# Modulation rows of two MLPs: four column blocks summed over partitions at once, on four column groups of the array, and turned

## The reference, cut to what matters

```python
mod_l = [m[:, None, :] for m in jnp.split(s_lat @ ada_w[i] + ada_b[i], N_MOD, axis=-1)]   # 1024 x 6144
...
h_lat = h_lat + mod_l[5] * _sq_relu_mlp(
    _modulate(_rmsnorm(h_lat, norm2_g[i]), mod_l[3], mod_l[4]), mlp_w1[i], mlp_w2[i])
...
mod = jax.nn.silu(c) @ w_ada[l] + b_ada[l]                                                # second block
```

## Time and profile before

| what | value |
|---|---|
| median of three runs | 2590.87 us (2590.12 to 2594.27) |
| the profiled execution, its own time | 2594.25 us |
| its span in the profile | 2592.4 us |
| mean granted clock of TensorE | 0.961 |
| TensorE busy | 2382.4 us, 92% |
| VectorE busy | 1006.2 us, 39% |
| ScalarE busy | 620.6 us, 24% |
| GpSimd busy | 112.4 us, 4% |
| HBM traffic | 592.5 MB, 229 GB/s over the span |

### The profile page before, as it was taken

The page is one execution under the profiler, slowest core; times in us unless marked ns, Lnnn a source line. Parts: engine busy times, 40 slices in busy tenths (PEclk is TensorE's granted clock), DMA queues, the critical chain, the costliest instruction groups (busy, mean ns, idle before and its releaser), DMA issues.

```text
span 2592.4 us, 23747 instructions
## 1 busy us (share of the span) xinstructions
PE 2382.4 (92%) x9961; PEld 1394.2 (54%) x9961; DVE 1006.2 (39%) x1616; ACT 620.6 (24%) x1002; POOL 112.4 (4%) x120
## 2 busy tenths in 40 slices
PE   5999988899999999999789979799898989989888
PEld 2445544588888788888667737333232323233222
DVE  4555463366663666564556372301111011101011
ACT  2112163333223333233446464110000000000000
POOL 2000000000000000000221312000000000000000
PEclk8999988999999999999899999899999999999999
DMA  9312330355553145550211203599999999999997
GB/s 352 105 65 81 109 118 0 114 182 190 174 184 128 49 163 195 195 179 33 89 49 33 94 29 130 215 427 429 431 430 432 430 431 431 431 430 432 429 431 316
DMA packets 121024, 594.04 MB, mean 229 GB/s; under 512 B 9346, under 2 KB 10880, under 8 KB 95318
## 3 DMA queue, kind: packets, MB, share of 16 engines
q1 hardware_dynamic: 117522, 583.23, 56.7%
q0 software_dynamic: 3088, 9.17, 1.0%
q10 hardware_dynamic: 308, 0.13, 0.0%
HBM read 590.37 MB, written 2.13 MB: 229 GB/s over the span
## 4 chain that ended last, share of the span: by engine, by line
PE 77%; DMA 12%; DVE 6%; ACT 3%; issue 1%; POOL 0%; DVEq 0%; ACTq 0%; POOLq 0%
PE PS L1150 15%; PE PS L840 9%; PE PS L842 9%; PE PS L841 9%; PE PS L656 8%; PE PS L891 5%; PE PS L149 5%; PE PS L1167 3%; DMA RING<-in_w_down_dram 3%; PE PS L1177 2%; PE PS L564 2%; DMA RING<-in_w_gate_dram 2%; PE PS L740 2%; DMA RB_a<-in_w_down_dram 2%; DMA RING<-in_w_up_dram 2%; PE PS L591 1%
## 5 line engine op out<-in xcount | busy, mean ns | idle before, releaser
L1150 PE MATMUL PS<-RING,HID_e 128*64 128x512 f32 x608 | 204.9, 607 | 9.1 <-DMA RING<-in_w_up_dram 4.7
L1150 PE MATMUL PS<-RB_a,HID_e 128*64 128x512 f32 x576 | 195.6, 598 | 5.2 <-DMA RB_a<-in_w_up_dram 4.5
L1150 PE MATMUL PS<-AT_g,HID_e 128*64 128x512 f32 x288 | 130.6, 601 | 5.1 <-DMA AT_g<-in_w_up_dram 4.2
L1150 PE MATMUL PS<-HID_e 128*64 128x512 f32 x288 | 130.8, 602 | 4.5 <-DMA HID_e<-in_w_gate_dram 2.7
L1150 PE MATMUL PS<-XT,HID_e 128*64 128x512 f32 x288 | 130.8, 602 | 4.3 <-DMA XT<-in_w_gate_dram 2.7
L2476 DVE TENSOR_TENSOR TMP<-TMP,PS 128x512 f32<-128x512 f32 x32 | 19.8, 683 | 284.6 <-PE PS L1150 284.6
L1167 PE MATMUL PS<-RING,HID_e 128*64 128x512 f32 x288 | 112.1, 656 | 13.0 <-DMA RING<-in_w_down_dram 13.0
L1696 ACT ACTIVATE PADS<-PS 128x512 f32<-128x512 f32 x8 | 4.8, 597 | 490.3 <-PE PS L149 490.3
L2484 DVE TENSOR_TENSOR HID_e<-PS,HID_e 128x512 f32<-128x512 f32 x16 | 10.3, 686 | 278.3 <-PE PS L1167 278.3
L1167 PE MATMUL PS<-RB_a,HID_e 128*64 128x512 f32 x304 | 107.3, 624 | 11.0 <-DMA RB_a<-in_w_down_dram 11.0
L1150 PEld LDWEIGHTS PS<-RING,HID_e 128*64 128x64 f32 x608 | 61.7, 139 | 97.7 <-issue 84.5
(11 more groups left out here) (448 smaller groups left out, 4712.9 us busy)
## 6 DMA issues: line engine op xcount, KB each, us to landing
RING<-in_w_gate_dram SPq DMA_DIRECT2D x19, 2048.0 KB, 22.0
RING<-in_w_up_dram SPq DMA_DIRECT2D x19, 2048.0 KB, 18.3
RB_a<-in_w_down_dram SPq DMA_DIRECT2D x19, 2048.0 KB, 21.6
RB_a<-in_w_gate_dram SPq DMA_DIRECT2D x18, 2048.0 KB, 22.4
RB_a<-in_w_up_dram SPq DMA_DIRECT2D x18, 2048.0 KB, 17.6
RING<-in_w_down_dram SPq DMA_DIRECT2D x18, 2048.0 KB, 21.9
RING<-in_mlp_w_dram SPq DMA_DIRECT2D x32, 1024.0 KB, 5.8
RB_a<-in_mlp_w_dram SPq DMA_DIRECT2D x32, 1024.0 KB, 5.3
```

The source lines that it names most:

```text
L1150: last = pe.matmul(b[64 * d:64 * d + 64, :], xv_[:, k, 64 * d:64 * d + 64], wv, start=k == 0, stop=k == 7)
```

## The change

For vectors 1 and 2, each block's tile of sums goes to its own row of `PADS` (`ada_sums`), so four blocks can stand finished side by side. After steps 8, 16 and 24 of each MLP, TensorE sums four blocks with four matmuls, each with 32 columns of ones as the stationary operand, a whole tile of 512 columns as the moving one, and 32 partitions of one PSUM bank as the target (`pe_ada_four`). ScalarE copies that bank to `ada_tmp` (`act_ada_row`), and after steps 9, 17 and 25 TensorE turns it with four transposes into the same bank (`pe_ada_turn`). VectorE adds the bias of all sixteen columns at once (`dve_ada_four`). Vector 0 is made as before. ScalarE's first step of a block no longer waits for the sum before it, only, from block 4 on, for the four that last read its row of `PADS`.

```diff
+        def ada_sums(which, cb):
+            return PADS[:, cb % 4, 0:512] if which else ada_tmp
...
+        def pe_ada_four(pe, w, which, g):
+            b = banks.take(w, ("ada_four", which, g), (V_ada, "add", which, 4 * g + 3))
+            w.wait_ge(*V_ada.at("acc", which, 4 * g + 3, 7))
+            for i in range(4):
+                last = pe.matmul(b[32 * i:32 * i + 32, :], ones[:, 0:32], ada_sums(which, i), start=True, stop=True)
+            last.then_inc(*T_ada.up("four", which, g))
+
+        def pe_ada_turn(pe, w, which, g):
+            w.wait_ge(*S_ada.at("row", which, g))
+            transposes(pe, banks.of("ada_four", which, g), [ada_tmp[:, 128 * j:128 * (j + 1)] for j in range(4)]).then_inc(
+                *T_ada.up("turn", which, g))
...
-                if jn % 2 and 0 < jn // 2 < 13:
-                    pe_ada_sum(pe, w, 1 + m, jn // 2 - 1)
+                if jn in (8, 16, 24):
+                    pe_ada_four(pe, w, 1 + m, jn // 8 - 1)
+                elif jn in (9, 17, 25):
+                    pe_ada_turn(pe, w, 1 + m, jn // 8 - 1)
...
-            w.wait_ge(*V_ada.at("add", 1, 1))
+            w.wait_ge(*V_ada.at("add", 1, 3))
...
-            else:
-                prev = (which, cb - 1) if cb else (which - 1, 11)
-                w.wait_ge(*T_ada.at("sum", *prev))
+            elif which == 0:
+                w.wait_ge(*T_ada.at("sum", 0, cb - 1))
+            elif cb > 3:
+                w.wait_ge(*T_ada.at("four", which, cb // 4 - 1))
...
+        def act_ada_row(act, w, which, g):
+            w.wait_ge(*T_ada.at("four", which, g))
+            if (which, g) == (1, 0):
+                w.wait_ge(*T_ada.at("sum", 0, 11))
+            elif g == 0:
+                w.wait_ge(*T_ada.at("turn", 1, 2))
+            else:
+                w.wait_ge(*T_ada.at("turn", which, g - 1))
+            act.activation(ada_tmp, banks.of("ada_four", which, g), ACT.Copy, bias=0.0, scale=1.0).then_inc(
+                *S_ada.up("row", which, g))
...
                 if jn and jn + 1 < 32:
                     act_split(act, w, m, jn + 1)
+                if jn in (8, 16, 24):
+                    act_ada_row(act, w, 1 + m, jn // 8 - 1)
...
+        def dve_ada_four(dve, w, which, g):
+            dst, bias = (mod1, vc("ada_b", 48 + 16 * g, 16)) if which == 1 else (mod2, vc("b_ada_2", 16 * g, 16))
+            w.wait_ge(*T_ada.at("turn", which, g))
+            sums = banks.of("ada_four", which, g).rearrange("p (j i m) -> p i j m", j=4, i=4)[:, :, :, 0]
+            dve.tensor_tensor(dst[:, 16 * g:16 * g + 16].rearrange("p (i j) -> p i j", j=4), sums,
+                              bias.rearrange("p (i j) -> p i j", j=4), ALU.add).then_inc(*V_ada.up("add", which, 4 * g + 3))
...
-                if 0 < s < 13:
-                    dve_ada_add(dve, w, 1 + m, s - 1)
+                if s in (4, 8, 12):
+                    dve_ada_four(dve, w, 1 + m, s // 4 - 1)
```

More of the change, by code:

```diff
@@ L585, in pe_ada_rows, with pe_ada_sum @@
             transposes(pe, b, [q[:, 128 * j:128 * (j + 1)] for j in range(4)]).then_inc(*T_set.up("ada_t"))
-        def pe_ada_sum(pe, w, which, cb):
-            b = banks.take(w, ("ada_sum", which, cb), (V_ada, "add", which, cb))
-            w.wait_ge(*V_ada.at("acc", which, cb, 7))
+        def pe_ada_sum(pe, w, cb):
+            b = banks.take(w, ("ada_sum", 0, cb), (V_ada, "add", 0, cb))
+            w.wait_ge(*V_ada.at("acc", 0, cb, 7))
             for j in range(4):
                 last = pe.matmul(b[:, j:j + 1], ada_tmp[:, 128 * j:128 * (j + 1)], ones[:, 0:1], start=True, stop=True)
-            last.then_inc(*T_ada.up("sum", which, cb))
+            last.then_inc(*T_ada.up("sum", 0, cb))
+        def pe_ada_four(pe, w, which, g):
[8 more added lines that the diff above has]
+                *T_ada.up("turn", which, g))
         def pe_norm(pe, w, n, N, *freed):
@@ L673, in pe_hyena @@
             part(2, 0, 1, 2, 3)
-            pe_ada_sum(pe, w, 0, 4)
+            pe_ada_sum(pe, w, 4)
             w.wait_ge(*D["dft"].all())
@@ L678, in pe_hyena @@
             part(0, 0, 1, 2)
-            pe_ada_sum(pe, w, 0, 5)
+            pe_ada_sum(pe, w, 5)
             for i in range(4):
@@ L707, in pe_hyena @@
             pe_norm_cols(pe, w, 1, 256)
-            pe_ada_sum(pe, w, 0, 6)
+            pe_ada_sum(pe, w, 6)
         def pe_rotate(pe, w, name, j):
@@ L731, in pe_qkv @@
                     pe_rotate(pe, w, "rk", 3)
-            pe_ada_sum(pe, w, 0, 7)
+            pe_ada_sum(pe, w, 7)
             w.wait_ge(*D["brow"].all())
@@ L742, in pe_qkv @@
                 if i % 2 == 0:
-                    pe_ada_sum(pe, w, 0, 8 + i // 2)
+                    pe_ada_sum(pe, w, 8 + i // 2)
             b = banks.take(w, ("lam",), (S_qkv, "lam"))
@@ L746, in pe_qkv @@
             pe.matmul(b[:, 0:2], ones[0:64, :], ST[0:64, 0:2], start=True, stop=True).then_inc(*T_qkv.up("lam"))
-            pe_ada_sum(pe, w, 0, 11)
+            pe_ada_sum(pe, w, 11)
         def pe_scores(pe, w, n):
@@ L1260, in act_ada @@
                 w.wait_ge(*T_set.at("ada", 7))
-            else:
-                prev = (which, cb - 1) if cb else (which - 1, 11)
-                w.wait_ge(*T_ada.at("sum", *prev))
+            elif which == 0:
+                w.wait_ge(*T_ada.at("sum", 0, cb - 1))
+            elif cb > 3:
+                w.wait_ge(*T_ada.at("four", which, cb // 4 - 1))
             w.wait_ge(*V_set.at("sil"))
             w.wait_ge(*ring.landed("ada", which, cb, 0))
-            act.activation(ada_tmp, ring.view("ada", which, cb, 0)[:, 0, :], ACT.Copy, bias=0.0, scale=scale).then_inc(
+            act.activation(ada_sums(which, cb), ring.view("ada", which, cb, 0)[:, 0, :], ACT.Copy, bias=0.0, scale=scale).then_inc(
                 *S_ada.up(which, cb))
+        def act_ada_row(act, w, which, g):
[8 more added lines that the diff above has]
+                *S_ada.up("row", which, g))
         def act_norm_root(act, w, n, src, N, fed):
@@ L1777, in dve_ada, with dve_ada_add @@
                 w.wait_ge(*(V_ada.at("acc", which, cb, k - 1) if k > 1 else S_ada.at(which, cb)))
[L1778 to L1788, removed]
+                dve.scalar_tensor_tensor(out=ada_sums(which, cb), in0=ring.view("ada", which, cb, k // 4)[:, k % 4, :],
+                                         scalar=sil[:, c0 + step * k:c0 + step * k + 1], in1=ada_sums(which, cb),
+                                         op0=ALU.mult, op1=ALU.add).then_inc(*V_ada.up("acc", which, cb, k))
+        def dve_ada_add(dve, w, cb):
+            w.wait_ge(*T_ada.at("sum", 0, cb))
+            dve.tensor_tensor(mod0[:, 4 * cb:4 * cb + 4, 0], banks.of("ada_sum", 0, cb)[:, 0:4], vc("ada_b", 4 * cb, 4),
+                              ALU.add).then_inc(*V_ada.up("add", 0, cb))
+        def dve_ada_four(dve, w, which, g):
[4 more added lines that the diff above has]
+                              bias.rearrange("p (i j) -> p i j", j=4), ALU.add).then_inc(*V_ada.up("add", which, 4 * g + 3))
         def gain(dve, sig, label, dst, scale, g):
@@ L1982, in dve_hyena @@
             part(2)
-            dve_ada_add(dve, w, 0, 4)
+            dve_ada_add(dve, w, 4)
             dve_kernel(dve, w)
@@ L1986, in dve_hyena @@
             part(0)
-            dve_ada_add(dve, w, 0, 5)
+            dve_ada_add(dve, w, 5)
             dve_waves(dve, w)
@@ L2004, in dve_hyena @@
             dve_norm(dve, w, 1, lambda k: ACX[:, k, :], 256)
-            dve_ada_add(dve, w, 0, 6)
+            dve_ada_add(dve, w, 6)
         def dve_rotate(dve, w, name, j):
@@ L2021, in dve_qkv @@
             dve_ada(dve, w, 0, 7)
-            dve_ada_add(dve, w, 0, 7)
+            dve_ada_add(dve, w, 7)
             dve_ada(dve, w, 0, 8)
             for cb in range(8, 11):
-                dve_ada_add(dve, w, 0, cb)
+                dve_ada_add(dve, w, cb)
                 dve_ada(dve, w, 0, cb + 1)
```

2 lines of the change are left out of this document (1 added, 1 removed).

## The result

The changed kernel takes 2581.1 us, the median of five runs (2576.99 to 2581.44), against 2590.87 us for five runs of the kernel before (2589.93 to 2594.27). The medians are 9.8 us apart. The means are 12.2 us apart, a ratio of 0.9953 with a 95% interval of 0.9938 to 0.9967, or 0.47% faster. The forecast was 2579.3 us in a range from 2575 to 2585.

What follows compares the result with a forecast made beforehand. TensorE was taken to bound the MLPs, its saving arriving in full: 22.8 us removed, 10.9 added, -11.9, plus 0.3 at VectorE's tight place, makes -11.6. From the median 2590.87 that forecasts 2579.3 us, range 2575 to 2585.

Steps and rivals of the forecast that it cites:

- What bounds: Both MLPs: TensorE sets the pace, the experts move earlier as a block, and the MLPs' saving counts in full.
- Removed: TensorE in the two MLPs: 24 sums at 0.95 us each go, 22.8 us, all on the path.
- Added, the four: TensorE, six times: four matmuls on four column groups, 0.86 plus 0.38 for tiling switches, 1.24 us; bounds 0.86 and 2.1.
- Added, the turn: TensorE, six times: four transposes, 0.43 us plus a sum's tail of 0.14, 0.57 us; bounds 0.43 and 0.95.
- Sum on TensorE: TensorE in both MLPs: 10.9 us added, 22.8 removed, net -11.9 us; bounds -15.1 and -4.5.
- Cover: ScalarE copies and following splits, VectorE's wider bias adds: cost 0, hidden by 5.8 us and 0.3 us of slack.
- The tight place: Steps 3, 11 and 19 of both MLPs: VectorE's margin is nil; 0.05 us each, 0.3 in all, bounds 0 and 1.8.
- A: Rival, chance 0.10: VectorE becomes the bound of the ph = 0 step pairs; with 4 us in all, 2583.0 us.
- B: Rival, chance 0.03: column groups enter one after another, 2.48 us per four matmuls instead of 1.24; 2586.7 us.
- C: Rival, chance 0.03: column groups don't overlap at all, 5.2 us per four matmuls with switches; slower, 2602.7 us.
- D: Rival, chance 0.05: later stretches, DMA-bound experts or a lower clock give the MLPs' saving back; about 2589 us.

Runs made afterwards that it cites:

- e1: Changed kernel without its six four-matmul sums, copies and turns, leaving blocks of vectors 1 and 2 unsummed: 2571.63 us, ratio 0.9921 to the kernel before.
- e5: Changed kernel plus one unused VectorE maximum behind the multiply-adds of steps 3, 11 and 19 of both MLPs: 2585.29 us, ratio 0.9975 to the kernel before.
- e2: Changed kernel plus four more matmuls behind each group of four, all writing the first column group: 2598.57 us, ratio 1.0027 to the kernel before.
- e3: Changed kernel with each group of four matmuls repeated on the same four column groups: 2585.97 us, ratio 0.9974 to the kernel before.
- e4: Changed kernel with sixteen one-column matmuls in a row replacing each group of four, no copy or turn: 2603.94 us, ratio 1.0050 to the kernel before.
- e8: Changed kernel with two blocks summed by eight small matmuls in a row after every fourth step instead: 2594.03 us, ratio 1.0002 to the kernel before.
- e11: Sixteen small matmuls per group, four behind each result bank of steps 9, 17 and 25, against the changed kernel's fours: 2593.03 us, 0.9998 to before.
- e9: Sixteen small matmuls per group, four behind each result bank of steps 8, 16 and 24, against the changed kernel's fours: 2624.72 us, 1.0130 to before.

## Why the prediction was right

- *What bounds:* TensorE paces the MLPs, and what it saves there arrives at the end. Shown by the time from the first MLP's start to the end, which follows the MLPs' length within 2.0 us in all eleven runs (13.9 for 12.6 in the changed kernel). The first load of the experts goes out 11.8 us earlier, where 11 to 12 were said.
- *Removed:* a sum was put at 0.95 us, 22.8 in all. e1 gives 0.93 and 22.4.
- *Added, the four:* put at 1.24, measured 1.20 in the timeline. The 0.18 us put on for draining and slower matmuls behind was a little too much.
- *Added, the turn:* put at 0.57, measured 0.46: the tail of a sum that I added to the 0.43 of the earlier trace rows was hardly there. The Trainium skill's 275 ns for a transpose (TensorE: Matmul & The Clock Gate, PE-mode transpose) would have made four of them 1.1 us, by the prediction's estimate. A record here lasts 272 ns, much like the page's figure, but the records overlap: four take 0.46 us in this stream.
- *Sum on TensorE:* -11.9 forecast, -12.6 in the profile (1.63 for a four with its turn instead of 1.81).
- *Cover:* the copies, the splits behind them and the wider bias adds cost nothing. The first split behind a four starts at 599.25, 1.7 us behind the step's end at 597.54, where 1.9 was said. The weights are complete at 603.48, 5.9 us behind it; the prediction gave 6.3, though its own terms add up to 6.1. A bias add is 168 ns, at the low bound.
- *The tight place:* the cost put on it, 0.3 us, is not seen, and its nil margin is. At step 3, one of the six places that lost their cover, the split ends at 551.49 + 2.28 = 553.77; the weight load that needs it starts 0.29 us behind the one ahead instead of 0.23, and its matmul is on time, 0.22 us behind the one ahead. That is the picture of the earlier trace rows. e5 shows that nothing is left there.

The changed kernel at step 3, VectorE, weight loads, matmuls:

```profile
551.49 2.28 DVE L2156 TENSOR_TENSOR WL_b<-RING,WH_b 128x2048 fp32r<-128x2048 f32 x1
...
553.54 0.19 PEld L860 LDWEIGHTS PS<-HH_b,WL_b 128*128 128x128 f32 x1
553.83 0.19 PEld L858 LDWEIGHTS PS<-HH_b,WH_b 128*128 128x128 f32 x1
...
553.77 0.39 PE L860 MATMUL PS<-HH_b,WL_b 128*128 128x512 f32 x1
553.99 0.40 PE L858 MATMUL PS<-HH_b,WH_b 128*128 128x512 f32 x1
```

- *The number:* the median fell by 9.8 us where the forecast said 11.6, while the means differ by 12.2 and the profiled pair by 12.9. The MLPs gave 1.0 us more than forecast, so the mechanism isn't short. The medians carry a scatter of 4 us from another stage (below), and five runs on each side don't average it out; that the median came within 1.8 us of the forecast is in part luck.
- *The rivals:* A by e1, B and C by e2 and e3, D by e1.

## What to carry to other kernels

A sum over partitions by one-column matmuls loads 128 columns of weights for each column moved: in e4's row of sixteen the weight loader was busy for all of 3.60 us. On column groups four tiles pass in the time of one (0.89 us against 3.43 / 4 = 0.86). The copy that this then needs can hide on an engine with room; the turn costs TensorE 0.46 us. Don't gather small matmuls in a row to save change-overs: e4 was worse than the scattered form, by the clock, though TensorE was never idle. And when time is taken off the bounding engine, look first at what stands just behind it: here VectorE has no margin left at every other pair of steps, and a further saving on TensorE within those steps should find it in the way, which no run tried.

## What the runs showed of the hardware that I had not expected

**A busy TensorE can lose its clock.** Sixteen float32 matmuls with one moving column each, 3.56 us in a row and counted as fully busy, were followed by some 3 us at the 1.2 GHz level at four of e4's six places and by 6.1 us at the other two. Eight in a row, 1.68 us, were not (e8), nor sixteen with twelve big matmuls between every four (e11), nor 4.4 us of float32 matmuls with 512 moving columns on 32 stationary ones (e2). So whether TensorE counts as busy in the profile doesn't tell whether it keeps its clock. Which property of the sixteen matters, their one moving column or their 128 stationary ones, stays open: no other moving size was tried in such a row.

**The scatter of the whole seems to be made ahead of the MLPs.** Runs of one kernel spread over 4 to 9 us. In the profiles, the first MLP starts anywhere from 491.3 to 496.9 us, though nothing ahead of it differs between the kernels, and everything behind it keeps its length within about 2 us, once the change of the MLPs is taken off. The stretch from 330 to 400 us, in attention, goes with it; here it is for the changed kernel (first MLP at 496.9), the kernel before (495.9), e4 (492.5) and e9 (491.3), with the granted clock third from the end:

```profile
330.00:400.00 70.00, 59.43 (x240) 34.74 (x239) 44.16 (x75) 42.50 (x88) 0.00 (x0) 0.84 0.19 70
```
```profile
330.00:400.00 70.00, 58.89 (x248) 34.25 (x246) 45.84 (x75) 43.23 (x90) 0.00 (x0) 0.88 0.20 75
```
```profile
330.00:400.00 70.00, 58.56 (x244) 34.12 (x245) 46.34 (x79) 42.81 (x89) 0.00 (x0) 0.90 0.18 65
```
```profile
330.00:400.00 70.00, 57.55 (x244) 33.24 (x243) 46.46 (x79) 42.54 (x89) 0.00 (x0) 0.93 0.19 70
```

The higher the clock granted there, the earlier the MLP starts; the other eight profiles fall in line, from 0.84 (496.9) to 0.90 (492.8). These are profiles of different kernels, one each; that the runs of one kernel differ for the same reason is inferred. Attention leaves TensorE idle in between, and it is given the lower level for more or less of the stretch; what decides how much was not tried. For a change of a few us in this kernel, the length of the stage that it touches is the better measure than the whole.
